# Seven more sets of 128x128 transposes taken off TensorE, in a two-block fp32 kernel

## What is computed

```
# first block
h = rmsnorm(x); proj = h @ w_in
q, ff, fb, i, gate, b, c, hc = split(proj)      # eight parts, 1024 wide each
y_rec = rmsnorm(hgrn_fwd + hgrn_bwd) * silu(gate)   # gated recurrence, 8 heads of 128
y_conv = b * conv3(c * hc)
x = x + concat(y_rec, y_conv) @ w_out
h2 = rmsnorm(x); x = x + (silu(h2 @ w_g) * (h2 @ w_u)) @ w_down
x = rmsnorm(x)
# second block; the six ada parts come from silu(c) @ w_ada + b_ada
h = rms(x) * (1 + sc1) + sh1
c_q, c_kv, k_pe, q_sb, k_sb, v_sb, gl_a, gl_b = split(h @ w_in)
y_a = latent attention(rms(c_q) @ w_uq, rms(c_kv) @ w_ukv, k_pe)
y_b = stick-breaking attention(q_sb, k_sb, v_sb)
merged = sigmoid(gl_a) * (y_a @ w_mla) + sigmoid(gl_b) * (y_b @ w_sb)
x = x + gt1 * (merged @ w_out)
h2 = rms(x) * (1 + sc2) + sh2; x = x + gt2 * ffn(h2)
```

## Time and profile before

| | |
|---|---|
| median of three runs | 2438.17 us (2436.59 to 2438.81) |
| the profiled execution | 2439.6 us, its span 2437.7 us |
| PE, weight loads of PE | 2426.1 us (100%), 2125.3 us (87%) |
| DVE | 1794.8 us (74%) |
| ACT | 1411.3 us (58%) |
| DMA, mean | 239 GB/s |
| 128x128 transposes on PE (line 664) | 242 |
| copies of 32x256 squares on ACT into `two` (line 1035) | 432, 403 ns each |

### The profile page before, as it was taken

How to read it: one execution, slowest core, us unless ns; L and a number is a source line. 1 busy time by engine, 2 the same in 40 slices (tenths; PEclk the granted TensorE clock), 3 DMA queues, 4 the chain that set the end, 5 groups by cost and what they waited for, 6 DMA issues and landing times. The chain is left out here.

```text
span 2437.7 us, 29441 instructions
## 1 busy us (share of the span) xinstructions
PE 2426.1 (100%) x11540; PEld 2125.3 (87%) x11540; DVE 1794.8 (74%) x2231; ACT 1411.3 (58%) x1980; POOL 26.0 (1%) x27
## 2 busy tenths in 40 slices
PE   9999999999999999999999999999999999999999
PEld 8898888888888888888888888888888888888888
DVE  7888798877778778786676667797778775555565
ACT  7647645756554456655766754465656564355643
POOL 0000000000000000000010000000000000000000
PEclk9999999999999999999999999999999999999999
DMA  8656666777778877786455447886577776556554
GB/s 305 241 195 234 232 217 247 255 292 267 272 271 311 298 275 276 262 292 223 170 185 179 158 172 247 304 282 235 178 277 279 276 279 209 198 203 206 200 205 147
DMA packets 83321, 582.38 MB, mean 239 GB/s; under 512 B 9712, under 2 KB 10096, under 8 KB 13552
## 3 DMA queue, kind: packets, MB, share of 16 engines
q1 hardware_dynamic: 83040, 580.39, 67.2%
q10 hardware_dynamic: 144, 0.12, 0.0%
HBM read 578.36 MB, written 2.11 MB: 238 GB/s over the span
## 5 line engine op out<-in xcount | busy, mean ns | idle before, releaser
L1418 DVE TENSOR_TENSOR wlo<-raw,whi 128x1024 fp32r<-128x1024 f32 x885 | 1078.5, 1222 | 559.6 <-ACT whi L994 555.5
L994 ACT CAST whi<-raw 128x1024 fp32r<-128x1024 f32 x885 | 926.2, 1048 | 754.6 <-PE bank L959 742.8
L957 PE MATMUL bank<-whi,hH 128*128 128x512 f32 x2528 | 967.9, 383 | 1.9 <-DVE wlo L1418 1.4
L958 PE MATMUL bank<-wlo,hH 128*128 128x512 f32 x2528 | 958.1, 379 | 0.0
L959 PE MATMUL bank<-whi,hL 128*128 128x512 f32 x2528 | 958.1, 379 | 0.0
L957 PEld LDWEIGHTS bank<-whi,hH 128*128 128x128 f32 x2528 | 477.9, 189 | 69.9 <-DVE wlo L1418 2.2
L959 PEld LDWEIGHTS bank<-whi,hL 128*128 128x128 f32 x2528 | 477.8, 189 | 67.9
L958 PEld LDWEIGHTS bank<-wlo,hH 128*128 128x128 f32 x2528 | 478.0, 189 | 65.6
L1924 DVE SCALAR_TENSOR_TENSOR adacc<-raw,stat,adacc 128x512 f32<-128x512 f32 x360 | 269.7, 749 | 6.8
L957 PE MATMUL bank<-whi,aH 128*128 128x512 f32 x704 | 267.1, 379 | 0.1
L958 PE MATMUL bank<-wlo,aH 128*128 128x512 f32 x704 | 266.8, 379 | 0.0
(11 more groups left out here) (331 smaller groups left out, 1516.9 us busy)
## 6 DMA issues: line engine op xcount, KB each, us to landing
raw<-in_w_gu_dram SPq DMA_DIRECT2D x176, 1024.0 KB, 4.9
raw<-in_w_ada_dram SPq DMA_DIRECT2D x96, 1024.0 KB, 4.9
raw<-in_w_down_dram SPq DMA_DIRECT2D x88, 1024.0 KB, 4.9
raw<-in_w_in_dram SPq DMA_DIRECT2D x60, 1024.0 KB, 4.8
raw<-in_w_in2b_dram SPq DMA_DIRECT2D x56, 1024.0 KB, 4.8
raw<-in_w_out_dram SPq DMA_DIRECT2D x32, 1024.0 KB, 4.9
raw<-in_w_in2a_dram SPq DMA_DIRECT2D x8, 1024.0 KB, 4.9
raw<-in_w_mla_dram SPq DMA_DIRECT2D x8, 1024.0 KB, 5.5
```

The lines of the kernel that those rows point to most:

```text
L957: e.matmul(o, xh[:, kt, sl], pairs(wh, i), start=k == 0, stop=False)
L958: e.matmul(o, xh[:, kt, sl], pairs(wl, i), start=False, stop=False)
L994: e.copy(whi[i][:, :, :], raw[u % RAW][:, 2 * hf:2 * hf + 2, :]).then_inc(*ev("act_hi", c, 0))
L1418: e.tensor_tensor(wlo[i][:, :, :], raw[u % RAW][:, 2 * hf:2 * hf + 2, :], f(whi[i][:, :, :]), ALU.subtract).then_inc(*ev("dve_lo", c, 0))
```

## The change

- **Seven things are turned the far way**: `fb 0`, `h 1`, `out 3`, `sb 3`, `latent 0`, `latent 1`, and the gated output of hgrn 0 (`hturn`). PE's instructions for them go. The squares of the latents lie in `gl1` and `gl2` and their features in `qn`; those of hgrn 0 in `TB` and `Kx`.
- **Paces**: `out 3` and `sb 3` take 4 copies on ACT and 4 on DVE a slot (settled at t = 4), `fb 0` and `h 1` 3 and 1 (settled at t = 6), the latents 3 and 0 two slots later than others (`lag`), hgrn 0 three a slot on ACT at u = 35 to 40.
- **hgrn 0 starts three slots later** (H0[0] = end of `fb 0` + 9) and lasts until u = 43.
- **Ada**: in `mla` and `sb` one unit per four weight units instead of per two, and in `out2` one per two. By the plan, the blocks `mla` and `sb` have 4 ada units instead of 8 and `out2` has 4; everything before `mla` and after `out2` keeps its place. The small matmul of column 19 goes from slot 606 to slot 622.

```
-        every_of = {"out": 4, "fgate": 3, "fup": 3, "fdown": 2, "gl": 2, "mla": 2, "sb": 2}
+        every_of = {"out": 4, "fgate": 3, "fup": 3, "fdown": 2, "gl": 2, "mla": 4, "sb": 4, "out2": 2}
...
-                elif b.kind in ("gl", "mla", "sb"):
+                elif b.kind in ("gl", "mla", "sb", "out2"):
...
-        H0 = [pl.end("fb", g) + 6 for g in range(2)]
+        H0 = [pl.end("fb", 0) + 9, pl.end("fb", 1) + 6]
...
-        FAR = (("fup", None), ("sb", 3), ("out", 3), ("heads", None), ("q", None), ("ff", None), ("h", 1), ("b", 1))
+        FAR = (("fup", None), ("sb", None), ("out", None), ("heads", None), ("q", None), ("ff", None),
+               ("h", None), ("b", 1), ("fb", 1), ("latent", None))
...
         def pace(b):
+            if b.kind in ("out", "sb") and b.arg[0] == 3:
+                return 4, 4
+            if b.kind == "fb" or b.kind == "h" and b.arg[0] == 1:
+                return 3, 1
...
+        def lag(b):
+            return 2 if b.kind == "latent" else 0
...
 # PE, hgrn
-                elif u in (35, 36):
+                elif u in (35, 36) and g == 1:
 # PE, left_here
                 elif b.kind == "out" and b.arg == (0,) and i == 0 and m == 0:
-                    if kt < 8:
+                    if kt < 4:
+                        e.wait_ge(*on("dve_low", "hturn", kt // 2))
+                    elif kt < 8:
...
-                    e.wait_ge(*side_read(pl.at["latent", 0 if b.kind == "uqr" else 1].index, ci))
+                    e.wait_ge(*on("dve_low", pl.at["latent", 0 if b.kind == "uqr" else 1].index, ci))
...
 # ACT, hgrn
+                elif g == 0 and 35 <= u < 41:
+                    if u == 35:
+                        for m in range(2):
+                            e.wait_ge(*on("dve_turned", "hturn", m))
+                    for k in range(3 * u - 105, min(3 * u - 102, 16)):
+                        ins = e.copy(*quadrant(*mixed_way(), *divmod(k, 4)))
...
+                elif g == 0 and u in (41, 42):
+                    if u == 41:
+                        e.wait_ge(*on("act_moved", "hturn"))
+                    for k in (2 * u - 82, 2 * u - 81):
+                        ins = e.activation(mH[:, k, :], mixed_way()[0][:, k, :], ACT.Copy, bias=0.0,
+                                           scale=vc("hgrn_norm_w", k))
...
 # DVE, hgrn
+                elif g == 0 and u == 34:
+                    for m in range(2):
+                        e.wait_ge(*on("dve_hgrn", g, "gated", m))
+                    for m in range(2):
+                        e.transpose(mixed_way()[1][:, m, :], T2[0][:, m, :]).then_inc(*ev("dve_turned", "hturn", m))
+                elif g == 0 and u in (42, 43):
+                    e.wait_ge(*on("act_half", "hturn", u - 42))
+                    for k in (2 * u - 84, 2 * u - 83):
+                        ins = e.scalar_tensor_tensor(mL[:, k, :], mixed_way()[0][:, k, :], vc("hgrn_norm_w", k),
+                                                     f(mH[:, k, :]), ALU.mult, ALU.subtract)
```

More of the change, by code:

```diff
@@ L599, in between @@
                 return gl[0][:, :, :] if b.arg == ("ks", 1) else T2[1 - b.index % 2][:, :, :]
-            k0 = 8 if (b.kind, b.arg[0]) == ("ff", 0) else 12
+            if b.kind == "latent":
+                return gl[1 + b.arg[0]][:, :, :]
+            k0 = 8 if b.kind in ("ff", "fb") and b.arg[0] == 0 else 12
             return way[k0][:, :, :]
@@ L622, in pieces, with quadrant, scaled_halves, mixed_way @@
             return [divmod(k, 4) for k in range(first, min(first + (na if who == "act" else nd), 16))]
+        def quadrant(features, rows, q, i):
+            d = features[32 * q:32 * q + 32, :, :].rearrange("p k (m i c) -> p m i k c", m=2, i=4)
+            r = rows[32 * i:32 * i + 32, :, :].rearrange("p m (k q c) -> p m q k c", k=4, q=4)
+            return d[:, :, i, :, :], r[:, :, q, :, :]
         def piece(b, q, i):
-            d = features_at(b)[32 * q:32 * q + 32, :, :].rearrange("p k (m i c) -> p m i k c", m=2, i=4)
-            r = between(b)[32 * i:32 * i + 32, :, :].rearrange("p m (k q c) -> p m q k c", k=4, q=4)
-            return d[:, :, i, :, :], r[:, :, q, :, :]
+            return quadrant(features_at(b), between(b), q, i)
+        def lag(b):
+            return 2 if b.kind == "latent" else 0
+        def scaled_halves(b):
+            if b.kind == "out":
+                return hH, hL, 4 * b.arg[0], "ffn_norm_w"
+            return ((cqH, cqL), (ckH, ckL))[b.arg[0]] + (0, ("g_q_latent", "g_kv_latent")[b.arg[0]])
+        def mixed_way():
+            return Kx[:, 1, :].rearrange("p (k s) -> p k s", k=4), TB[:, :].rearrange("p (m f) -> p m f", m=2)
         def halves_of(b):
@@ L1048, in block_side @@
                         e.copy(mH[:, k0:k0 + 4, P * m:P * m + P], v4(T[5 + m])).then_inc(*ev("act_half", b.index, m))
-                elif is_far(b) and kind == "out" and t in (8, 9):
-                    half, k0 = t - 8, 4 * b.arg[0]
+                elif is_far(b) and kind in ("out", "latent") and t - lag(b) - settled(b) in (0, 1):
+                    half, (hi, _, k0, gname) = t - lag(b) - settled(b), scaled_halves(b)
                     if half == 0:
@@ L1059, in block_side @@
                     e.copy(halves_of(b)[0], features_at(b)).then_inc(*ev("act_half", b.index))
-                elif is_far(b) and t >= 2 and kind != "out":
+                elif is_far(b) and t - lag(b) >= 2 and kind != "out":
                     return
@@ L1498, in block_side @@
                 t -= late0(b)
-                if is_far(b) and t == 1:
-                    turned(b)
-                elif is_far(b) and 2 <= t < settled(b) and pace(b)[1]:
+                if is_far(b) and 2 <= t < settled(b) and pace(b)[1]:
                     if t == 2:
@@ L1508, in block_side @@
                         ins.then_inc(*ev("dve_moved", b.index))
+                if is_far(b) and t - lag(b) == 1:
+                    turned(b)
                 elif is_far(b) and kind in ("fup", "sb") and t == settled(b) + 1:
@@ L1512, in block_side @@
                     e.tensor_tensor(lo, features_at(b), f(hi), ALU.subtract).then_inc(*ev("dve_low", b.index))
-                elif is_far(b) and kind == "out" and t in (9, 10):
-                    half, k0 = t - 9, 4 * b.arg[0]
+                elif is_far(b) and kind in ("out", "latent") and t - lag(b) - settled(b) in (1, 2):
+                    half, (hi, lo, k0, gname) = t - lag(b) - settled(b) - 1, scaled_halves(b)
                     e.wait_ge(*on("act_half", b.index, half))
                     for k in (2 * half, 2 * half + 1):
-                        ins = e.scalar_tensor_tensor(hL[:, k0 + k, :], features_at(b)[:, k, :], vc("ffn_norm_w", k0 + k),
-                                                     f(hH[:, k0 + k, :]), ALU.mult, ALU.subtract)
+                        ins = e.scalar_tensor_tensor(lo[:, k0 + k, :], features_at(b)[:, k, :], vc(gname, k0 + k),
+                                                     f(hi[:, k0 + k, :]), ALU.mult, ALU.subtract)
                     ins.then_inc(*ev("dve_low", b.index, half))
@@ L1649, in block_side @@
                         *ev("dve_mean", "latent", i))
-                elif kind == "latent" and t == 5:
+                elif kind == "latent" and t == 5 and not is_far(b):
                     i = b.arg[0]
@@ L1751, in turned @@
                         e.wait_ge(*on("dve_x1", b.index, m))
+                    elif b.kind == "latent":
+                        e.wait_ge(*on("act_lat", b.index, m))
                     else:
```

41 lines of the change are left out of this document (24 added, 17 removed).

## The result

The change makes the kernel slower: 2443.86 us median of ten runs (2443.49 to 2445.42) against 2438.34 (2436.59 to 2438.89) for the kernel before, a ratio of 1.0026 with a 95% interval of 1.0017 to 1.0034. The range held it; the sign and the forecast of no change did not hold.

The account below looks back on a forecast made before the run. PE was taken as bounding the kernel, busy all the time at 2.4 GHz. Terms -6.2 - 6.6 + 3.5 + 1.6 + 1.2 + 4.4 + 1.8 = -0.3 us gave 2437.9 us from the 2438.2 median; 8-in-10 range 2430 to 2446.5.

Parts of the forecast that it names:

- -6.2 for 56: Seven places turned far: 56 transposes leave PE at 0.11 us each, all on the path, -6.2 us.
- The ada term: mla and sb: fewer ada units relieve DVE, so PE's waits and the clock fall go; -6.6 us, bounds 0 to -6.6.
- fb 0: Far turning of fb 0: copies fit ACT's nearly empty slots; 0 us, ends 0 and +0.5.
- slow steps: Behind visit 613: the wait is followed by nine steps at the lower clock, +1.8 us.
- hgrn 0, visit 78: Visits 70 to 78: DVE and ACT fall behind, visit 78's low 4.4 late; taken as +3.5 us, ends 0 and 6.
- h 1, slot 129: Slot 129: added DVE work delays the gating that PE turns; +1.6 us, ends 0 and 2.5.
- out 3, visits 166 and 167: Visits 166, 167: DVE's squares and copies make each `hL` late; +1.2 us, ends 0 and 1.7.
- sb 3, visit 613: Visit 613: `hL` comes late behind squares, copies and two ada pairs; +4.4 us, ends 1 and 5.
- Latents: Two latents turned far: ACT's 2.3 us a slot is covered by two slots of `lag`; 0 us.
- No big wait stayed hidden: Rival: waits at hgrn 0 or sb 3 never appear; one hidden 2431 to 2434, chance 0.17; both or all 0.10.
- The clock did not fall in visits 70 to 78: Rival: clock falls among these waits, 2443 to 2445 us; chance 0.22, shared with some wait at its upper end.
- The price by duration: Rival: each transpose off PE saves its 274 ns duration, 15.3 us for 56, giving 2428.8 us; chance 0.03.

Follow-up runs that it names:

- c2_pairs: Changed kernel with three ada units moved by two slots (125 to 127, 163 to 165, 610 to 612): 2440.41 us.
- b1_fbpe: Changed kernel with fb 0 turned on PE again and hgrn 0 begun six slots after it, as before the change: 2444.64 us.
- c4_lat: Changed kernel with only the two latents far and the new ada places; other turnings on PE, hgrn 0 starting as before: 2431.08 us.
- d2_out3: `c4_lat` with out 3 turned far too and the ada unit of slot 163 moved by two slots: 2430.14 us.
- d3_hg: `d2_out3` with hgrn 0's output far too, squares in slot 68, copies in slots 70 to 80: 2429.67 us.
- a4_hg1: Changed kernel with hgrn 0's 16 copies one a slot (slots 68 to 83) instead of three, halves in slots 84 to 86: 2442.52 us.
- c1_hg: Changed kernel with hgrn 0's squares one slot later (68), copies in slots 70 to 80, halves in 81, low halves in 83 and 84: 2440.31 us.
- c3_both: Changed kernel with the edits of both `c1_hg` and `c2_pairs`: 2436.93 us, ratio to the kernel before 0.9995.
- d4_lump: Changed kernel with all 16 copies of hgrn 0 in ACT's slot 68 instead of three a slot: 2448.17 us.

## Why the prediction was wrong

*What bounds the kernel, and the two gains: right.* PE's pace, 0.11 us a transpose and -6.2 for 56 came out at -6.1. The ada term, -6.6, was -6.9 in the trace; made alone it gave 6.5 by the start of `out2` and 5.3 by the medians.

*The places of the losses: right.* Each of the four stood where it was said, behind the engine that was said. Elsewhere the losses were 0.6 us in fb 0 and 0.3 before visit 392.

*Their sizes: wrong, all to the same side.* The sum had two gains of 12.8 against four losses of 12.5, so the sizes set the sign. The step that failed is the sizing of these four: 12.5 was forecast, 16.4 measured, 1.6 of the difference at hgrn 0, 1.2 at `sb 3` with its slow steps, 0.7 at `out 3` and 0.4 at `h 1`. What was late, and when, compares like this:

| | releaser late, as reckoned | in the trace | PE lost |
|---|---|---|---|
| hgrn 0, visit 78 | 4.4, taken as 3.5 | 5.0 | 5.1 |
| h 1, slot 129 | 1.6 | 1.9 | 2.0 |
| out 3, visits 166 and 167 | 0.5 and 0.7 | 1.0 and 0.5 | 1.9 |
| sb 3, visit 613 | 4.4 | 4.9 | 5.0 |

*hgrn 0: the reckoning was nearly right, and I cut it.* DVE's slots 64 to 67 took 16.0 us, as reckoned, and ACT's from there to the cast of chunk 78 took 24.6, as reckoned:

```profile
195.67 1.23 DVE L1463 TENSOR_TENSOR wlo<-raw,whi 128x1024 fp32r<-128x1024 f32 x1 [2.35 <-ACT whi L1023]
...
210.37 1.29 DVE L1940 STREAM_TRANSPOSE TB<-two 128x512 f32<-128x512 f32 x2
...
235.28 1.03 ACT L1023 CAST whi<-raw 128x1024 fp32r<-128x1024 f32 x1
236.34 1.23 DVE L1463 TENSOR_TENSOR wlo<-raw,whi 128x1024 fp32r<-128x1024 f32 x1 [1.10 <-ACT whi L1023]
```

Only the start was off: DVE began slot 64 at 2.0 us behind visit 63 (193.69) and not at 1.5 (in the first row it had waited for a cast). The last low ends 43.9 behind visit 63, where visit 78 was due at 38.9: 5.0 late. The 0.9 that I took off, since the same reckoning had been 1 to 2 us too late elsewhere, was an error, and the other 0.7 is the start and what a late start of PE costs on top. ACT waited for 0.20 us in between, for squares of `q`, and never for PE, so the six waits are pieces of one debt; they are not six costs to be added to it. That the idle time, 3.35, is near the 3.5 is chance.

*sb 3: mis-sized.* The reckoning has DVE go through slots 609 to 612 without a wait. In the trace it waits 0.51 us for a cast that stands behind ACT's four copies, and `hL` ends 15.2 behind visit 609 (1664.15) where 14.7 was reckoned and 10.4 was due:

```profile
1670.52 1.22 DVE L1463 TENSOR_TENSOR wlo<-raw,whi 128x1024 fp32r<-128x1024 f32 x1 [0.51 <-ACT whi L1023]
...
1678.17 1.22 DVE L1557 TENSOR_TENSOR hL<-two,hH 128x1024 fp32r<-128x1024 f32 x1
```

The slow steps took 2.4 in place of 1.8, the one value that the trace before had. By `c2_pairs`, 1.9 us of the wait was the ada pairs of `out2`.

*What a late start costs on top: left out.* At visits 70 to 78 PE starts 0.06 us after the end of the low and loses 0.10 in the next step; at visits 166, 167 and 613 it starts 0.15 after the end of `hL`, and at the first two of these it loses 0.07 in the next step. The earlier trace rows already held the second part (1623.43 to 1623.75, 0.32 for a step). That is 0.1 to 0.2 for each place, and twice that at `out 3`, where two halves are waited for one by one: some 0.8 of the 3.9 in all.

*fb 0: missed.* It was costed at nothing, with a bound of +0.5. A wait of 0.16 before visit 28 and waits too short for the list behind it made +0.6 of the 0.9 that its transposes gave. That DVE's squares and copy ahead of the lows make them is argued; with `fb 0` on PE again (`b1_fbpe`) visits 28 to 30 lose 0.5 less.

*The base.* The terms were read in an execution of 2439.6 us and counted from the median of 2438.2. That adds about 1.0 to the miss: 5.0 by the terms, 6.0 by the medians.

*Two misreadings.* The plan takes four of the eight ada units from all of `mla` and `sb` together, not "a block"; in visits 595 to 606 DVE lost 4.7 us of work. And of the 3.0 us in five waits for `wlo`, 1.4 stood before visits 1 and 2 and could not go. The -6.6 came from visit starts and so did not suffer.

*Latents: right.* Their cover held, and `c4_lat` has the whole 1.75.

*The rivals.* No big wait stayed hidden. The clock did not fall in visits 70 to 78 (granted 1.00 in the window from 209 to 240 us): the waits there were at most 0.80. The price by duration (274 ns a transpose) would have needed 15 us; the trace gave 6.1. The Trainium skill's rule for transposes (VectorE: DVE Perf Modes, "Rules for kernel authors"), that TensorE is the place for 128x128 ones where a PSUM destination will do, is borne out by the changed kernel at visits 70 to 78, slot 129, visits 166 and 167 and visit 613, each of which lost more than its 0.9; at the latents, at `out 3` once an ada unit had made room (`d2_out3`), and at hgrn 0 with squares and copies placed elsewhere (`d3_hg`), the measurement speaks against it, since the helpers had time there.

## What to carry to other kernels

Work that is taken off a saturated engine is worth its marginal time there, and it costs nothing only in slots where the helpers' queues have room: price each place by itself and keep those where nothing waits. A change that bundles a gain of scheduling with a gain of work has to be taken apart before either is believed: here two lines gave 5.3 to 6.5 us, and four of the seven sets gave all of it back and more. When gains are set against losses of the same size, a few tenths in each decide the sign: reckon how late the last releaser of a place is against the start that was due, leave the figure as it comes out unless a row of that very place says otherwise, and count gains from the execution in which they were read.

## What the runs showed of the hardware

A wait costs PE its idle time plus 0.23 to 0.27 us, alike for idle times of 0.20 and of 1.00 us. 0.16 of it is the part of the matmul before (0.38 us long, 0.216 from start to start) that would have lain under the next one; 0.10 is lost in the step behind a wait for a low, 0.07 in that behind the waits of visits 166 and 167.

In the profiled executions slow steps (0.43 us instead of 0.22, granted clock 0.50 in the window above) followed each wait of 2.20 us and more and, behind the first two visits, none of 1.76 and less. How long they lasted did not go with the wait: a wait of 4.86 to 4.88 before visit 613 was followed by 2.1 us lost in `a4_hg1`, 2.4 in the changed kernel and 3.0 in `c1_hg`; one of 3.0 by 1.8 in `c2_pairs` and 3.0 in `c3_both`; one of 5.06 by 2.0 in `d4_lump`. Each kernel has one trace, so whether this is chance or hangs on the kernel is not shown; differences of a microsecond between kernels that have such a wait should not be given a cause. Between 1.76 and 2.20 no run has a wait.

A unit of weights read two slots later delayed the loads behind it: in `c2_pairs` the next load of `w_out` was issued 3.9 us after the start of visit 613, where in the changed kernel it was 2.4 us before it; ACT then waited 9.40 us for a DMA, and PE 1.49.

What made the wait of 0.36 us before visit 392 stays open. The seven kernels that show it have both `fb 0` and hgrn 0's output far; the others lack at least one of them.
